# Five edits at the stage borders of a two-block transformer kernel: the gate's sigmoid one chunk ahead, the neighbourhood output chunk by chunk, the first retention scores one piece later, the last scaling shared with GpSimd, the root tables loaded early

## The reference

```python
# end of first_block
e = p[i] @ w_ple[i]
x = x + e * jax.nn.sigmoid(x @ w_ple_gate[i])

# second_block
h = rms_norm(x, norm_mix[l])
na_q, na_k, na_v, r_q, r_k, r_v, r_g = jnp.split(h @ w_in[l], splits, axis=-1)
na_out = neighbourhood_attention(na_q, na_k, na_v, na_rpb[l])
ret = bidirectional_retention(rotary(r_q), rotary(r_k) * RET_QK_DIM ** -0.5, r_v, ...)
ret_out = jax.nn.silu(r_g) * head_group_norm(ret, ret_norm_gain[l])
x = x + jnp.concatenate([na_out, ret_out], axis=-1) @ w_out[l]
h = rms_norm(x, norm_mlp[l])
x = x + jnp.square(jax.nn.relu(h @ w_up[l])) @ w_down[l]
return rms_norm(x, norm_final)
```

## Time and profile before

| what | value |
|---|---|
| median of 3 runs | 1334.03 us (1333.63 to 1334.16) |
| the profiled execution's own time | 1333.72 us |
| its span, first to last instruction | 1331.9 us |
| PE busy | 1294.6 us (97%) |
| DVE busy | 816.8 us (61%) |
| ACT busy | 641.6 us (48%) |
| POOL busy | 149.9 us (11%) |

### The profile page before, as it was taken

The page is one execution under the profiler, slowest core; times in us unless marked ns, Lnnn a source line. Parts: engine busy times, 40 slices in busy tenths (PEclk is TensorE's granted clock), DMA queues, the critical chain, the costliest instruction groups (busy, mean ns, idle before and its releaser), DMA issues.

```text
span 1331.9 us, 16618 instructions
## 1 busy us (share of the span) xinstructions
PE 1294.6 (97%) x6092; PEld 1073.6 (81%) x6092; DVE 816.8 (61%) x1578; ACT 641.6 (48%) x1242; POOL 149.9 (11%) x133
## 2 busy tenths in 40 slices
PE   8999999999999999999999999999999999999996
PEld 7888888877888888888787777888878888888885
DVE  5769989786664556346777877588544333344344
ACT  6777666554444443233444655476453243242342
POOL 0011111000110011000002100022211021020110
PEclk9988999999999999999999999999999999999998
DMA  7211110333322332332322221432232323232321
GB/s 261 88 33 47 33 32 28 124 86 96 97 86 87 111 103 83 107 95 80 111 79 79 86 72 49 123 111 76 72 99 92 103 87 103 87 105 90 105 80 63
DMA packets 63584, 118.20 MB, mean 89 GB/s; under 512 B 7696, under 2 KB 10128, under 8 KB 63248
## 3 DMA queue, kind: packets, MB, share of 16 engines
q1 hardware_dynamic: 62352, 113.48, 27.7%
q10 hardware_dynamic: 1152, 3.67, 0.8%
HBM read 115.02 MB, written 2.10 MB: 88 GB/s over the span
## 4 chain that ended last, share of the span: by engine, by line
PE 79%; DVE 12%; ACT 5%; issue 3%; DMA 0%; DVEq 0%; ACTq 0%; SPq 0%
PE bank L538 24%; PE bank L539 23%; PE bank L540 23%; DVE wl L1769 2%; PE bank L733 1%; DVE pp L1938 1%; PE bank L616 1%; PE bank L617 1%; PE bank L618 1%; ACT wh L1162 1%; DVE ptl L1961 1%; PE bank L719 1%; PE bank L720 1%; DVE pp L1955 1%; ACT sqr L1181 1%
## 5 line engine op out<-in xcount | busy, mean ns | idle before, releaser
L1769 DVE TENSOR_TENSOR wl<-raw,wh 128x512 fp32r<-128x512 f32 (+2 forms) x360 | 270.8, 765 | 341.6 <-ACT wh L1162 340.8
L1162 ACT ACTIVATE wh<-raw 128x512 fp32r<-128x512 f32 (+1 forms) x398 | 241.2, 619 | 291.3 <-PE bank L540 279.9
L538 PE MATMUL bank<-AH,wh 128*128 128x512 f32 x832 | 331.1, 398 | 4.1 <-DVE wl L1769 3.1
L539 PE MATMUL bank<-AL,wh 128*128 128x512 f32 x832 | 326.9, 393 | 0.0
L540 PE MATMUL bank<-AH,wl 128*128 128x512 f32 x832 | 326.7, 393 | 0.0
L538 PE MATMUL bank<-BH,wh 128*128 128x512 f32 x624 | 249.4, 400 | 2.9 <-DVE wl L1769 2.9
L539 PE MATMUL bank<-BL,wh 128*128 128x512 f32 x624 | 245.5, 393 | 0.0
L540 PE MATMUL bank<-BH,wl 128*128 128x512 f32 x624 | 245.2, 393 | 0.0
L538 PEld LDWEIGHTS bank<-AH,wh 128*128 128x128 f32 x832 | 157.6, 189 | 41.0 <-DVE wl L1769 4.1
L540 PEld LDWEIGHTS bank<-AH,wl 128*128 128x128 f32 x832 | 157.2, 189 | 36.1
L539 PEld LDWEIGHTS bank<-AL,wh 128*128 128x128 f32 x832 | 157.4, 189 | 33.1 <-issue 0.2
(11 more groups left out here) (298 smaller groups left out, 1667.0 us busy)
## 6 DMA issues: line engine op xcount, KB each, us to landing
raw<-in_w_dn SPq DMA_DIRECT2D x104, 256.0 KB, 2.7
raw<-in_w_gu SPq DMA_DIRECT2D x88, 256.0 KB, 2.6
raw<-in_w_up SPq DMA_DIRECT2D x64, 256.0 KB, 2.6
raw<-in_w_nsa SPq DMA_DIRECT2D x16, 256.0 KB, 2.6
raw<-in_w_pg SPq DMA_DIRECT2D x16, 256.0 KB, 2.6
raw<-in_w_naq SPq DMA_DIRECT2D x16, 256.0 KB, 2.6
nbi<-in_na_bias ACTq DMA_DIRECT2D x8, 448.0 KB, 3.3
raw<-in_w_swa SPq DMA_DIRECT2D x10, 256.0 KB, 2.6
```

The source lines that it names most:

```text
L538: t.matmul(o, w, xh, start=start, stop=False, skip_group_check=skip)
L539: t.matmul(o, w, xl, start=False, stop=False, skip_group_check=skip)
L1162: a.activation(W[i % NW].h[:, 0:n], RAW[i % NRAW][:, 0:n], ACT.Copy).then_inc(*s_wh.up(i))
L1769: v.tensor_tensor(w.l[:, 0:n], RAW[i % NRAW][:, 0:n], w.h[:, 0:n], ALU.subtract).then_inc(*s_wl.up(i))
```

## The change

1. **Gate.** ScalarE takes the sigmoid of chunk c+1 before it makes the high part of chunk c, and converts the chunk's weight piece before both. VectorE makes that piece's low part before the chunk's own low part.
2. **Retention.** TensorE runs the piece `w_mid` 0 before `s_part(0, 0)` instead of after it.
3. **Neighbourhood output.** The weights are repacked: a piece holds all four input chunks for one output chunk, so an output chunk ends with every piece. Conversion of weights, addition to x and splitting alternate, chunk by chunk. The sum of squares on TensorE moves from ahead of `w_up` piece 7 to ahead of piece 3, and the root stands after four pieces' conversions instead of seven.
4. **End.** The factor is spread into a second bank by four more matmuls, ScalarE copies it to SBUF (`r_bc`), and GpSimd multiplies chunks 6 and 7 by it, VectorE only 0 to 5. SP stores in the order 0, 1, 6, 2, 3, 7, 4, 5. `add_square` of a chunk now stands right behind its addition, so seven squares are summed before the last chunk.
5. **Root tables.** The one-column activation that brings in the square root's table is moved ahead of the square of chunk 7 in three places (`y1`, `y2`, `x5`), and dropped in a fourth (`x1`), where the table is in place already.

```diff
 # tensor
+            half_of("w_mid", 0, ("gate", 0))
             s_part(0, 0)
-            half_of("w_mid", 0, ("gate", 0))
             s_part(0, 1)
...
-            for i in range(2):
-                keys = [("xo", 4 * i + g) for g in range(4)]
-                product("w_out_na", 4 * i, A, na_out, [0, 1, 2, 3], 4, 1, keys)
-                for key in keys:
-                    bank.give(key)
+            for c in range(8):
+                product("w_out_na", c, A, na_out, [0, 1, 2, 3], 1, 4, [("xo", c)])
+                bank.give(("xo", c))
...
-                            {7: lambda: sums("x4", r_bc[:, :], s_adg.at(("x4", 7)))} if gi == i == 0 else None)
+                            {3: lambda: sums("x4", r_bc[:, :], s_adg.at(("x4", 7)))} if gi == i == 0 else None)
...
             soon_back("x5")
+            b, free = bank.take(("bk2", "x5"))
+            e.wait_ge(*free)
+            for i in range(4):
+                c = slice(P * i, P * i + P)
+                m = t.matmul(b[:, c], ones[:, :], tmp.ap(("x5", "d"))[:, c], start=True, stop=True)
+            m.then_inc(*s_st.up(("bk2", "x5")))
+            bank.give(("bk2", "x5"))
 # scalar
+                if c == 7:
+                    root_table("y1")
                 out1(c)
...
+            root_table("y2")
             down_out(2, 7)
...
+                gate_of_chunk(2 * m)
                 for c in range(2 * m, 2 * m + 4):
-                    z, s = bank.ap(("z", c)), tmp.ap(("sg", c))
-                    e.wait_ge(s_mm.at(("o", ("z", c))), *tmp.before(("sg", c)))
-                    a.activation(s[:, 0:T], z[:, :], ACT.Sigmoid).then_inc(*s_fn.up(("sg", c)))
-                    bank.read(("z", c), (s_fn, ("sg", c)))
+                    hi(WHERE["w_pg", 4 * m] + 8 + c - 2 * m + 4)
+                    if c < 2 * m + 3:
+                        gate_of_chunk(c + 1)
                     split("x3", c, B[c], chunk(X, c), g2mix[:, c:c + 1], s_dv.at(("x3", c)), piece("w_dn1t", 7))
                     square("x3", c, chunk(X, c))
-                    hi(WHERE["w_pg", 4 * m] + 8 + c - 2 * m + 4)
...
-            for i in range(2):
-                ahead("w_out_na", 4 * i, 4)
-                for g in range(4):
-                    c = 4 * i + g
-                    split("x4", c, B[c], chunk(X, c), g2mlp[:, c:c + 1], s_sv.at(("xo", c)), s_mm.at(("p", WHERE["w_naq", 15])))
-                    square("x4", c, chunk(X, c))
-                behind("w_out_na", 4 * i + 3)
+            for c in range(8):
+                behind("w_out_na", c)
+                split("x4", c, B[c], chunk(X, c), g2mlp[:, c:c + 1], s_sv.at(("xo", c)), s_mm.at(("p", WHERE["w_naq", 15])))
+                square("x4", c, chunk(X, c))
...
-                        ahead("w_up", k0, 7)
+                        ahead("w_up", k0, 4)
                         root(("x4",))
...
             soon("x5")
+            e.wait_ge(s_st.at(("bk2", "x5")))
+            a.activation(r_bc[:, :], bank.ap(("bk2", "x5"))[:, :], ACT.Copy).then_inc(*s_cp.up(("r2", "x5")))
 # vector
+                    lo(WHERE["w_pg", 4 * m] + 8 + c - 2 * m + 4)
                     split("x3", c, B[c], chunk(X, c), g2mix[:, c:c + 1])
-                    lo(WHERE["w_pg", 4 * m] + 8 + c - 2 * m + 4)
...
+            for c in range(8):
+                x_add(c, ("xo", c), ("xo", c), s_sv.at(("xr", c)))
+                behind("w_out_na", c)
+                split("x4", c, B[c], chunk(X, c), g2mlp[:, c:c + 1])
...
-                        if gi == 3 and c:
-                            add_square("x5", c - 1)
+                        if gi == 3 and i:
+                            lo(WHERE["w_dn2", k0 + 2 * g + 1] + 4)
+                        if gi == 3 and c < 7:
+                            add_square("x5", c)
                     behind("w_dn2", k0 + 7)
             soon("x5")
-            for c in range(8):
+            for c in range(6):
 # gpsimd
+            for c in (6, 7):
+                e.wait_ge(s_cp.at(("r2", "x5")), s_cp.at(("xg", c)))
+                g.tensor_tensor(chunk(X, c), chunk(X, c), r_bc[:, :], ALU.mult).then_inc(*s_gp.up(("out", c)))
 # sync
-            for c in range(8):
-                e.wait_ge(s_dv.at(("out", c)))
+            for c in (0, 1, 6, 2, 3, 7, 4, 5):
+                e.wait_ge(s_gp.at(("out", c)) if c > 5 else s_dv.at(("out", c)))
```

27 lines of the change are left out of this document (13 added, 14 removed).

## The result

The changed kernel took 1319.45 us (median of four executions, profiled one included, 1318.16 to 1322.01), the kernel before beside it 1333.83 us (four, 1330.51 to 1334.16): ratio 0.990, 95% interval 0.9877 to 0.9923. The profiled execution of the changed kernel is its slowest, 1322.01 us, with a span of 1320.2 us and a granted clock of 0.992.

A forecast was written before the change was run, and what follows sets the result against it. TensorE, busy 97% of the span, was taken as the bound, with its waits and the lower clock behind them to win. Gate -5.2, retention +0.2, output and `w_up` -5.0, `y2` -0.2, end +0.7: -9.5, so 1324.2 us, range 1320.6 to 1327.6.

The forecast's parts named there:

- Gate, -5.2: Gate: TensorE's 3.11 us wait for piece 15's low part and the lower clock behind it go, 5.2 us gained.
- the 3.4 to 4.2 that I gave: Gate: the chunk cycle in us expected in the changed kernel's profile, against 5.04 before.
- the rivals that kept one: Gate wait only shortened (1325.2 to 1326.9 us) or `w_up` pause stays (1328.2); chance 0.18 together.
- Retention, +0.2: Retention: the first scores' wait moves to `v_part(0, 0)` as a 2.6 us pause with lower clock; 0.2 us lost.
- Output and `w_up`, -5.0: Neighbourhood output and first `w_up` product: both pauses and the lower clock behind the second go, 5.0 us gained.
- `y2`, -0.2: Root at `y2`: the root's lateness behind the sums goes, 0.2 us gained, ends 0 and 0.4.
- The end, +0.7: End: sums about 1.0 us earlier, but sharing with GpSimd loses 1.7 at the lower clock; 0.7 us slower.
- that case: End with the clock up: both spreadings take half the time and the end comes 1.2 us earlier.
- my 1 to 2 us: End: expected gap in the stores before the third, while SP stands for GpSimd's chunk 6.
- Three of three such pauses were followed by the lower level: Argument that the clock falls behind the pause at `v_part(0, 0)`, from pauses of 2.11, 2.26 and 3.11 us.
- that rival: The clock holds at `v_part(0, 0)`, at the end, or both: 1320.6 to 1322.5 us; chance 0.25.
- The slower rival: Chunk-by-chunk output repeats the gate's serial chain at 5.04 us a chunk: 1339 us; chance 0.03.

The follow-up runs named there:

- copy_split: low_first without the shared final scaling, and ScalarE's four copies of the last rotated tile parted two and two; 1319.00 us, 0.9897 of the kernel before.
- before_again: The kernel before, unchanged, run once more in the follow-up series; 1331.74 us.
- low_first: Changed kernel with the first scores' rounding and low parts ahead of other work on ScalarE and VectorE; 1318.95 us, 0.9896 of the kernel before.
- after_again: The changed kernel, unchanged, run once more in the follow-up series; 1319.95 us, 0.9906 of the kernel before.
- sum_late: Changed kernel with the sum of x4's squares behind eight pieces of `w_up` again, output still chunk by chunk; 1326.71 us, single execution.
- gate_sigmoid: Changed kernel with the gate's weights converted behind the chunk's split again, sigmoid still a chunk ahead; 1329.01 us, single execution.
- gate_only: The kernel before with edit 1 (gate) alone; 1326.54 us, 0.9964 of the kernel before.
- scores_later: low_first without the shared final scaling, and `w_mid` 2 ahead of the third scores on TensorE; 1319.09 us, 0.9897 of the kernel before.

## Why the prediction was wrong, point by point

- **Gate, -5.2: right.** 5.35 us in the profile, 5.35 alone. The cycle was mis-sized: 4.5 us, outside the 3.4 to 4.2 that I gave. I let GpSimd stretch an instruction by 0.7 us; the product, which started almost with GpSimd's addition, lost 1.1. Piece 15 came at 703.97 us, against my late estimate of 703.7. In the end no wait was left in the gate and in `w_up`, so the rivals that kept one did not come true. Of the two things that edit 1 does, I had not separated the one that works (the weights' place) from the one that doesn't (the sigmoid).
- **Retention, +0.2: right in kind.** The wait moved to `v_part(0, 0)` as forecast. The pause is 3.2 us, not 2.6: measured from x3's sum, the product starts 1.1 us earlier than before, where I had 1.5. What I got wrong is that I took this chain as fixed. Much of it is queue order on ScalarE and VectorE, and copy_split won 2.6 us there.
- **Output and `w_up`, -5.0: right, a little small.** 5.45 us: the gap of 0.31 us at 956.3 went too, as in my upper end of 5.3. With the sum at its old place the pause of 2.37 us is back, so this half is shown; the clock's 1.7 us behind it is real only in some executions. Against before_again, where it was missing, the same edit is worth 3.9 us.
- **`y2`, -0.2: right** (378.73 to 378.53).
- **The end, +0.7: the mechanism was right, the clock was not.** The column sums of chunk 7 start 1.83 instead of 2.77 us behind the last matmul, 0.94 sooner, as forecast, and sharing costs 0.7 us of that at full clock and 1.6 at the lower level (the run without it). The changed kernel's profile met full clock: -1.1, where I had -1.2 for that case. The other case was never met cleanly, since the time depends on when the lower level begins: 16.15 us with it from 3.7 us behind the last matmul on (low_first), 15.82 in after_again, and for the end as it was 15.49 with it from 4.8 us on (before) but 16.28 from 2.8 us on (before_again). The DMA engines' stand is 0.6 us at full clock, so my 1 to 2 us did not show either. The end is 1.8 us of the 2.2 by which the sum of the profiles differs from mine.
- **The level: the step that failed.** "The profiled execution took 1333.72 us ... That gives 1324.2 in the trace's terms". The sum was set off from three executions within 0.5 us of each other, as if the kernel took that time. In 52 later ones its median is 1331.4 us, and 1334 is in its upper fifth. The level goes with the clock: the 12 of them with a mean granted clock of 0.986 or 0.987 have a median of 1333.8 us, the 25 with 0.990 and more one of 1330.2, and the profiled execution had 0.986. 1331.4 - 11.7 = 1319.7, and 1319.45 was measured: of the 4.75 us that I was off, about 2.6 are this level and 2.2 the sum. The second part is less firm than the first, since the other pair of profiles gives -8.5 instead of -11.7; the medians themselves (1331.4 against 1319.45 and 1319.95) differ by 11.5 to 12. The range failed for the same reason: its low end held only two places for the clock, both in the changed code, while the start of the kernel alone moves by 6 us between executions.
- **"Three of three such pauses were followed by the lower level"** was too small a sample. Over all profiles, pauses of 3.1 to 3.3 us were followed by it in each of eleven cases, for 2.9 to 3.4 us in eight and for 5.7 to 6.0 us in three (after_again, sum_late, gate_sigmoid); those of 2.1 to 2.3 us in six of nine. The same 2.11 us pause cost 1.5 us in one execution and nothing in the other. The Trainium skill (TensorE: Matmul & The Clock Gate, Part 1) calls the observation free-running; the runs agree in that the same pause costs or not. I gave that rival 0.25; it came true at the end and not at `v_part`, and by itself it gave no less than 1320.6 us.
- **The slower rival** is excluded: the output's cycle is 2.74 us, TensorE's own.

Open: what decides in an execution whether the lower level comes, and what made gate_only's matmuls 1.9% slower at a granted clock of 1.00. Four of the 52 executions of the kernel before took 1339 to 1341 us; whether they are of this kind no trace shows.

## What to carry to other kernels

Cut two profiles at marks and compare stretches: here the gate's edit was worth 5.3 to 5.4 us in every pair, while executions of the same code spread by 8 us (changed) and 13 us (before). A stretch that has a pause of 2 us in it holds the clock's chance too (3.9 or 5.4 us for the output), so compare stretches with the clock beside them. Before setting a forecast off from a few executions that agree, ask how much of their time hangs on the clock in code that is not touched, and let the range take that in. When a wait moves to the next instruction, read the queues in front of its producer before calling the chain fixed; a weight conversion or a copy that nobody needs yet is often in it.

## What the runs showed of the hardware

- A VectorE instruction of 128x512 that reads two tiles from SBUF and starts while GpSimd adds or subtracts such tiles gets through 0.55 us after GpSimd has ended, whether it began 0.1 us (product, 1.79 us) or 0.5 us (conversion, 1.42 us) after it. The 16 traces have 630 such conversions and products, and all end 0.54 to 0.56 us behind GpSimd. A low part `BL` that began 0.56 us before GpSimd's addition took its 0.75 us. VectorE's additions with one input from PSUM stayed at 0.68 to 0.69 us beside GpSimd. The Trainium skill (GPSIMD Engine Reference, SBUF interfaces) says that such contention comes with two SBUF inputs, and the trace agrees.
- The lower level also comes without a pause just before it (788.1 to 791.5 us in scores_later, 795.8 to 799.2 in gate_only). What TensorE did before both was sixteen one-column matmuls, 1.84 us, that ended some 1.5 us before the clock fell; in the other 14 profiles the same matmuls were not followed by it.
- TensorE ran 320 us long with a matmul every 0.2333 instead of 0.2289 us in gate_only, with a granted clock of 1.00 in the records. The same distance stands in all 16 profiles for shorter stretches, such as 24 to 29 us from the value projection on. In the kernel before, six matmuls apart and 1.40 us:

```profile
720.09 0.39 PE L617 MATMUL bank<-wh,BL 128*128 128x512 f32 x1
721.49 0.39 PE L617 MATMUL bank<-wh,BL 128*128 128x512 f32 x1
```
